# Hybrid decoder step on 8 cores: three small loads moved to ACT's queue, one tile load moved to GpSimd's queue, the second half of the down products placed after the last up product, and the last tile finished in halves

## The reference, cut to what matters

```python
def block(x, pool_ctx, pos, run_mlstm, norm1, w_in, b_gate, w_pool, pool_scale, head_gain, w_out, norm2, w_up, w_down):
    u, q, k, v, o, ig, lf = mixer_inputs(x, norm1, w_in, b_gate)      # rmsnorm(x) @ w_in, 1024 -> 2568
    u_ext = jnp.concatenate([pool_ctx.astype(u.dtype), u], axis=1)
    pool_out = pool_mix(u_ext, pos, w_pool, pool_scale)               # moving averages over 2, 4, 8, 16 rows
    h, mstate = run_mlstm(q, k, v, ig, lf)                            # matrix memory, chunk after chunk
    x = x + mixer_output(pool_out, h, o, head_gain, w_out, x.dtype)
    x = x + channel_mixer(x, norm2, w_up, w_down)                     # square(relu(rmsnorm(x) @ w_up)) @ w_down, 1024 -> 4096 -> 1024
    return x, u_ext[:, -POOL_CTX:], mstate
...
    y_prompt = rmsnorm(xp[:, N_META:], norm_f)
    y_sample = rmsnorm(xs, norm_f)
```

## Time and profile before

| | us |
|---|---|
| median of 3 runs (lowest to highest) | 813.78 (812.28 to 815.24) |
| the profiled execution, its own time | 813.62 |
| its span on the slowest core, core 5 | 812.6 |
| spans of the eight cores | 804.5 to 812.6 |
| PE busy on core 5 | 761.5 (94% of the span) |
| DVE, ACT, POOL busy | 425.9, 363.4, 156.9 |

### The profile page before, as it was taken

One profiled execution on the slowest core, in us unless ns is written; L12 is line 12 of the kernel. 1 busy time (PEld: TensorE's weight loads), 2 busy tenths in 40 slices (PEclk: granted clock), 3 DMA queues, 4 the chain that ended last, 5 costly groups with the idle time before them and its releaser, 6 DMA issues.

```text
span 812.6 us, 16660 instructions; the slowest of 8 cores (804.5 to 812.6 us)
## 1 busy us (share of the span) xinstructions
PE 761.5 (94%) x6707; PEld 529.1 (65%) x6707; DVE 425.9 (52%) x952; ACT 363.4 (45%) x867; POOL 156.9 (19%) x241
## 2 busy tenths in 40 slices
PE   0799899999999999999999799959999999999996
PEld 0477677878778788878798577628744444444442
DVE  0755886768768648768566665134323242421211
ACT  3455695776878536868637554103310010101011
POOL 6532430333312311202311301010000110000000
PEclk9999999999999999999999999979999999999999
DMA  8999994344344332332226799963355555553401
GB/s 165 175 199 178 184 189 94 92 85 92 91 112 99 62 103 58 87 117 79 66 78 92 159 187 280 224 138 105 99 214 186 202 200 202 164 187 118 186 34 53
DMA packets 35716, 110.43 MB, mean 136 GB/s; under 512 B 3415, under 2 KB 6855, under 8 KB 31654
## 3 DMA queue, kind: packets, MB, share of 16 engines
q1 hardware_dynamic: 21446, 63.64, 26.4%
q0 software_dynamic: 9504, 28.67, 22.1%
q10 hardware_dynamic: 4688, 17.04, 5.8%
HBM read 96.41 MB, written 39.64 MB: 167 GB/s over the span
## 4 chain that ended last, share of the span: by engine, by line
PE 81%; DMA 9%; DVE 5%; issue 2%; ACT 1%; POOL 1%; SPq 0%; POOLq 0%; DVEq 0%; ACTq 0%
PE B L428 79%; DMA wdn<-w_down 5%; PE B L431 2%; DMA xdn<-w_down 2%; DMA gvec<-gcols 2%; DMA C0b<-sC 1%; DVE zt L437 1%; DVE ast L434 0%; DVE xn2T L434 0%; DVE rows L441 0%; DVE wsm L441 0%; DVE xnT L434 0%; DVE Pt L434 0%; SPq L422 0%; POOL Wa L448 0%
## 5 line engine op out<-in xcount | busy, mean ns | idle before, releaser
L428 PE MATMUL B<-xn2T,wup 128*128 128x256 bf16 (+1 forms) x2304 | 247.3, 264 | 0.0
L428 PE MATMUL B<-wdn,aTl 128*128 128x512 bf16 (+1 forms) x952 | 213.8, 382 | 9.1 <-DMA xdn<-w_down 9.1
L428 PEld LDWEIGHTS B<-xn2T,wup 128*128 128x128 bf16 x2304 | 203.7, 98 | 23.4 <-issue 0.4
L428 PEld LDWEIGHTS B<-wdn,aTl 128*128 128x128 bf16 (+1 forms) x952 | 93.7, 99 | 120.9 <-DMA xdn<-w_down 9.2
L434 DVE TENSOR_TENSOR xt<-xt,B 128x512 f32<-128x512 f32 (+1 forms) x68 | 46.6, 685 | 183.7 <-PE B L428 183.4
L434 DVE TENSOR_TENSOR ast<-rr 128x512 bf16<-128x512 f32 x132 | 97.2, 736 | 74.6 <-ACT rr L425 58.4
L425 ACT ACTIVATE rr<-B 128x512 f32<-128x512 f32 x132 | 78.3, 593 | 112.5 <-PE B L428 66.9
L425 ACT ACTIVATE junk<-xt 128x1024 bf16<-128x1024 f32 (+1 forms) x17 | 18.0, 1057 | 196.3 <-DVE xt L434 196.3
L428 PE MATMUL B<-w_out_sb,mixT 128*128 128x512 bf16 (+1 forms) x272 | 64.2, 386 | 0.0
L448 POOL TENSOR_TENSOR kz<-ktm,wsm 64x512 bf16<-64x512 bf16 x16 | 16.7, 1059 | 167.2 <-PE B L428 155.5
L425 ACT ACTIVATE xn<-xt 128x1024 bf16<-128x1024 f32 (+2 forms) x34 | 35.8, 1052 | 22.7 <-DVE xt L434 20.2
(11 more groups left out here) (196 smaller groups left out, 932.3 us busy)
## 6 DMA issues: line engine op xcount, KB each, us to landing
aTd<-ast SPq DMA_DIRECT2D x32, 512.0 KB, 4.1
aTl<-aTd SPq DMA_DIRECT2D x16, 1024.0 KB, 4.9
wup<-w_up POOLq DMA_DIRECT2D x8, 1024.0 KB, 36.8
x2d<-xt SPq DMA_DIRECT2D x16, 512.0 KB, 3.8
xt<-x2d SPq DMA_DIRECT2D x16, 512.0 KB, 3.8
yp<-xt ACTq DMA_DIRECT2D x16, 512.0 KB, 2.6
wdn<-w_down POOLq DMA_DIRECT2D x7, 1024.0 KB, 14.0
xt<-xp SPq DMA_DIRECT2D x13, 512.0 KB, 4.8
```

The costliest lines, as they stand in the source:

```text
L428: return lambda: nc.tensor.matmul(out, lhsT=lhsT, rhs=rhs, start=start, stop=stop)
```

## The change

The loads of `gvec`, `earl` and `rowc` go from SP's queue to ACT's, ahead of everything else there, with a one-element exponential (`warm`) behind the first of them, which pulls the load of ACT's function table to the start. The load of prompt tile 1 goes from the head of SP's queue to GpSimd's (`XSW` 1). A key `upend` is written by the last up products and read by every PE operation on blocks 4 to 7, and by the load of the third `aTl`. The load of `gfB` (the last norm's gains) reads `wdn5`, and the loads of `C0f` for `csu(e)` read `dn{e}`, the end of down product e. The last tile's norm, scaling and store are split in two column halves, with a second store on SP. `POOLP` goes from 10 to 40 and `OGP` from 0 to 60.

```diff
@@ -19,7 +19,7 @@
 EPS = 1e-6
 WIN = (2, 4, 8, 16)
 UPV = 1800
-PRE, FRONT, MID, TAIL, POOLP, OGP = -50, -50, 30, -150, 10, 0
+PRE, FRONT, MID, TAIL, POOLP, OGP = -50, -50, 30, -150, 40, 60
 NBC = 5
 LOG = None
 
@@ -516,6 +516,7 @@
         colS = sb("colS", [80, 24])
         decr = sb("decr", [4, 16]); msr = sb("msr", [4, 16]); mpr = sb("mpr", [4, 1])
         mix_end = base[0]
+        warm = sb("warm", [1, 2])
 
         eo = [t_off["wup2"][0]]
 
@@ -554,6 +555,7 @@
 
 
         bank = pl.newbank
+        G(-5, lambda: nc.gpsimd.memset(warm[:, 0:1], 1.0), [], ['warm'], 0.1)
 
         def bk(b): return 'V%d' % b
 
@@ -561,9 +563,10 @@
         pl.place('xt0m', *pl.span['xt0'])
         pl.split('xt0', 'xt0m')
         DMA(0, 'sp', xt[0][64:80, :], meta[:, :], [], ['xt0m'], 'meta', 64e3)
-        DMA(0, 'sp', earl[:], early[:, :], [], ['earl'], 'earl', 64e3)
-        DMA(0, 'sp', gvec[:], gcols[:, :], [], ['gvec'], 'gvec', 10e3)
-        DMA(0, 'sp', rowc[:], rowin[:, :], [], ['rowc'], 'rowc', 1e3)
+        DMA(-3, 'act', gvec[:], gcols[:, :], [], ['gvec'], 'gvec', 10e3)
+        DMA(-2, 'act', earl[:], early[:, :], [], ['earl'], 'earl', 64e3)
+        DMA(-1, 'act', rowc[:], rowin[:, :], [], ['rowc'], 'rowc', 1e3)
+        A(-4, act(warm[:, 1:2], warm[:, 0:1], AF.Exp), ['warm'], ['warm2'], 1.5)
 
         def memset(prio, ap, v, key, cost, R=()):
             G(prio, lambda: nc.gpsimd.memset(ap, v), list(R), [key], cost)
@@ -680,7 +683,7 @@
         def scan(out, d, init, op0, op1):
             return lambda: nc.vector.tensor_tensor_scan(out=out, data0=d, data1=d, initial=init, op0=op0, op1=op1)
 
-        XSW = {2: 2.5, 3: 4.2, 4: 5.2}
+        XSW = {1: 1.5, 2: 2.5, 3: 4.2, 4: 5.2}
 
         def xload(pos):
             i = pos - 1
@@ -1036,7 +1039,7 @@
                         fns = []
                         for k in range(8):
                             fns.append(mm(B[b][:, hf * 256:(hf + 1) * 256], w_up_sb[fo][:, k, (f % 8) * 128:(f % 8 + 1) * 128], xn2T[gs][:, k, :], k == 0, k == 7))
-                        P(pr, fns, ['xn2T%d0' % gs, 'xn2T%d1' % gs, 'wup%d0' % fo, 'wup%d1' % fo], [bk(b)], 8 * mm_cost(256))
+                        P(pr, fns, ['xn2T%d0' % gs, 'xn2T%d1' % gs, 'wup%d0' % fo, 'wup%d1' % fo], [bk(b)] + (['upend'] if g == 7 and fo == 3 and fp == 3 else []), 8 * mm_cost(256))
                     av = a[:].rearrange("p t f c -> p f t c")[:, 2 * fp:2 * fp + 2, :, :]
                     r_ = rc[0] % 2; rc[0] += 1
                     A(pr - UPV, act(rr[r_][:], B[b][:], AF.Relu), [bk(b)], ['rr%d' % r_], cA(512))
@@ -1053,7 +1056,7 @@
                 for fi in range(8):
                     for k in range(8):
                         fns.append(mm(B[b][:, fi * 64:(fi + 1) * 64], w_up_sb[fo][:, k, fi * 128:(fi + 1) * 128], xn2T[0][:, k, 0:64], k == 0, k == 7))
-                P(pr, fns, ['xn2T00', 'wup%d0' % fo, 'wup%d1' % fo], [bk(b)], 64 * 0.034)
+                P(pr, fns, ['xn2T00', 'wup%d0' % fo, 'wup%d1' % fo], [bk(b)] + (['upend'] if fo == 3 else []), 64 * 0.034)
                 av = a[:, 0, 0:4, :].rearrange("p f c -> p (f c)")
                 r_ = rc[0] % 2; rc[0] += 1
                 A(pr - UPV, act(rr[r_][:], B[b][:], AF.Relu), [bk(b)], ['rr%d' % r_], cA(512))
@@ -1127,12 +1130,12 @@
         NC = 3
         C0f = [pbt("C0f%d" % i, [128, 8, 128]) for i in range(NC)]
         kz = [pbt("kz%d" % i, [64, 4, 128], BF16) for i in range(2)]
-        DMA(2400, 'sp', gfB[:], norm_f.partition_broadcast(128), [], ['gfB'], 'gfB', 512e3)
+        DMA(2400, 'sp', gfB[:], norm_f.partition_broadcast(128), ['wdn5'], ['gfB'], 'gfB', 512e3)
 
         def csu(e, pr):
             s = e % NC
             ck = 'C0f%d' % s
-            DMA(pr - 200, 'act', C0f[s][:], sCv[:, 8 * e:8 * e + 8, :], [], [ck], 'L' + ck, 512e3)
+            DMA(pr - 200, 'act', C0f[s][:], sCv[:, 8 * e:8 * e + 8, :], ['dn%d' % e], [ck], 'L' + ck, 512e3)
             for jj in range(2):
                 j = 2 * e + jj
                 z = kz[j % 2]; zk = 'kz%d' % (j % 2)
@@ -1144,6 +1147,8 @@
                       [ck, 'decS', bk(b)], [ck], 0.35)
             DMA(pr, 'act', Csv[:, 8 * e:8 * e + 8, :], C0f[s][:], [ck], ['o_C_s%d' % e], 'S' + ck, 512e3)
 
+        for half in range(2):
+            pl.place('xo%d' % half, t_off['xt3'][0] + 2048 * half, t_off['xt3'][0] + 2048 * half + 2048)
         order = list(range(8)) + [SP] + list(range(8, 16))
 
         def loads(n):
@@ -1154,7 +1159,7 @@
                 av = aTl[a][:].rearrange("p f c -> p (f c)")[:, 0:2048].rearrange("p (f c) -> p f c", c=64)
                 DMA(pr - 200, 'sp', av, aTs[:, :, :], ['aTs'], ['aTl%d' % a], 'LaTl%d' % a, 512e3)
             else:
-                DMA(pr - 200, 'sp', aTl[a][:], aTd[t], ['aTd%d' % (t // 2)], ['aTl%d' % a], 'LaTl%d' % a, 1024e3)
+                DMA(pr - 200, 'sp', aTl[a][:], aTd[t], ['aTd%d' % (t // 2)] + (['upend'] if n == 2 else []), ['aTl%d' % a], 'LaTl%d' % a, 1024e3)
             nr = 64 if t == SP else 128
             DMA(pr - 190, 'sp', xb[n % 3][0:nr, :], x2d[128 * t:128 * t + nr, :], ['x2d%d' % t], ['xt%d' % (n % 3)], 'x%d' % (n % 3), 512e3)
 
@@ -1169,13 +1174,29 @@
                 av = a[:].rearrange("p f c -> p (f c)")[:, 0:2048].rearrange("p (f c) -> p f c", c=64)
             else:
                 av = a[:]
+            last = n == 16
+            s_ = st[n % 2]; sk = 'st%d' % (n % 2)
             for half in range(2):
+                hc = slice(half * 512, (half + 1) * 512)
                 b = bank('D')
                 for q in range(2):
                     P(pr, [mm(B[b][r_, :], av[:, f, r_], wdn[f // 4][:, f % 4, half * 512:(half + 1) * 512], f == 0, f == 31) for f in range(16 * q, 16 * q + 16)],
-                      [ak] + ['wdn%d' % u for u in range(4 * q, 4 * q + 4)], [bk(b)], 16 * mm_cost(512))
+                      [ak] + (['upend'] if q else []) + ['wdn%d' % u for u in range(4 * q, 4 * q + 4)], [bk(b)] + (['dn%d' % n] if half and q else []), 16 * mm_cost(512))
                 V(pr - 1000, vtt(x_[r_, half * 512:(half + 1) * 512], x_[r_, half * 512:(half + 1) * 512], B[b][r_, :], ALU.add), [xk, bk(b)], [xk], cV(512))
-            s_ = st[n % 2]; sk = 'st%d' % (n % 2)
+                if last:
+                    A(pr - 1000, act(junk[:, hc], x_[:, hc], AF.Square, accum_out=s_[:, 2 + half:3 + half]), [xk], ['junk', sk], 0.8)
+                    V(pr - 1000, vtt(xt[3][:, hc], x_[:, hc], gfB[:, hc], ALU.mult), [xk, 'gfB'], ['xo%d' % half], 0.6)
+                    if half == 0:
+                        V(pr - 1000, vts(s_[:, 4:5], s_[:, 2:3], 1.0 / D, ALU.mult, EPS, ALU.add), [sk], [sk], 0.15)
+            if last:
+                A(pr - 1000, act(s_[:, 5:6], s_[:, 3:4], AF.Ln, scale=1.0 / D, bias=s_[:, 4:5]), [sk], [sk], 0.21)
+                A(pr - 1000, act(s_[:, 5:6], s_[:, 5:6], AF.Exp, scale=-0.5), [sk], [sk], 0.21)
+                V(pr - 1000, vts(xt[3][:, 0:512], xt[3][:, 0:512], s_[:, 5:6], ALU.mult), ['xo0', sk], ['xo0'], 0.4)
+                A(pr - 1000, act(xt[3][:, 512:1024], xt[3][:, 512:1024], AF.Copy, scale=s_[:, 5:6]), ['xo1', sk], ['xo1'], 0.6)
+                for half, q in ((0, 'sp'), (1, 'act')):
+                    DMA(pr, q, yp[128 * t:128 * t + 128, half * 512:(half + 1) * 512], xt[3][:, half * 512:(half + 1) * 512],
+                        ['xo%d' % half], ['o_yp%d%d' % (t, half)], 'xo%d' % half, 256e3)
+                return
             A(pr - 1000, act(junk[r_, :], x_[r_, :], AF.Square, accum_out=s_[r_, 2:3]), [xk], ['junk', sk], 1.25)
             rstd(pr - 1000, s_, sk, 2, nr)
             V(pr - 1000, vstt(x_[r_, :], x_[r_, :], s_[r_, 3:4], gfB[r_, :], ALU.mult, ALU.mult), [xk, sk, 'gfB'], [xk], 1.25)
```

## The result

The changed kernel takes 802.55 us (median of four runs, 802.31 to 802.81) against 814.51 us for the kernel before, run beside it. The ratio is 0.9858, with an interval from 0.9837 to 0.9878: 12.0 us faster. 797 us were forecast. So the sign and most of the amount came as said, and 5.5 us are missing.

The account below looks back on a forecast made before the run. PE's work bounds the kernel nearly everywhere. 812.6 - 2.0 - 2.7 - 11.6 + 0.5 - 1.1 + 0.5 = 796.2 us, plus 1.0 us for the execution's own time, gives 797 us; range 790 to 807 us.

Parts of the forecast that it names:

- the forecast's own case: Whole kernel: the forecast as it stands, 797 us, own range 791 to 802 us; chance 0.62.
- rival (a): At the start of the down products: the store of `ast` takes the place of `xdn`; 803 to 809 us; chance 0.20.
- The start: Start of the kernel: earlier small loads bring `xnT` and `tt` sooner; 2.0 us gained, between 0 and 3.6.
- Rival (c): At the kernel's start: the small loads stay as slow as they were; 800 us; chance 0.10.
- The wait for `Pt`: Near 467 us: more PE work ahead of the wait cuts it; 2.7 us gained, between 0 and 3.4.
- The start of the down products: Up matmuls now precede the wait for `xdn`: 9.1 us of wait and 2.5 us of low clock go, 11.6 us gained.
- The store of `ast`: Between the last up products and down products: a late store may stop PE; 0.5 us lost, between 0 and 12.
- The tail: Last add to last store: less square and scaling behind the last product; 1.1 us gained, between 0.7 and 1.6.
- The new order elsewhere: From 110 us on: `POOLP` and `OGP` shift the engines' order; 0.5 us lost, between 0 and 5.
- rival (d): In every prompt tile: the new order makes PE wait at `Pt` or `mixh`; over 814 us; chance 0.05.

Follow-up runs that it names:

- the priorities back: Changed kernel with `POOLP` and `OGP` put back to 10 and 0: 798.73 us, ratio 0.9832.
- The down part alone: Kernel before with only `upend` and the conditions on the third `aTl`, `gfB` and `C0f` loads: 7.7 us faster, 9.7 us in the mean of the cores.
- the one with only the `C0f` condition: Changed kernel with `POOLP` and `OGP` at 10 and 0 and, of the three conditions on loads, only that on `C0f`: ratio 0.9814.
- The mark alone: Kernel before with `upend` on the last up products and second-half down products, no conditions on the loads: 806.6 us, ratio 0.9926.
- priorities alone: Kernel before with only `POOLP` and `OGP` changed, to 40 and 60: ratio 0.9993.
- the changed kernel less its down part: Changed kernel without `upend` and without the conditions on the third `aTl`, `gfB` and `C0f` loads: ratio 0.9988.

## Why the prediction was right, and where it was off

The 802.5 us lie inside the stated range of 790 to 807 us, but half a microsecond above the 802 us to which the forecast's own case reached, and below the 803 us at which rival (a) began. The largest term of the sum, the down products, and that of the start came nearly as said; what kept the time from 797 us is mostly one small term, the last one below.

**The start**, 2.0 us forecast: 2.6 us by the time, 1.6 us in the mean of the cores. Each step came within 1 us: `xnT` done at 11.5 us, the `wo` product from 13.8 us (forecast 14.4), `tt` at 18.8 us (19.4). The 1.5 us by which `wo` was to land sooner did not follow from their own numbers (4.8 us less 2 or 3 is 1.8 to 2.8 us), and it was 2.2 us (11.2 us for 13.4 us). Rival (c) is refuted by the 2.1 us of `gvec`. What I had not seen is that the clock takes part of it back. PE, which began earlier and then waited for `wo` and `wk`, ran the next products at the lower of its two levels (1.2 GHz), as their durations show; from 20 to 45 us the granted clock is 0.80, for 0.93 before. After the change:

```profile
22.05 2.31 PE L428 MATMUL B<-xnT,wk 128*128 128x80 bf16 x32 [3.44 <-DMA wk<-w_in]
...
29.23 3.11 PE L428 MATMUL B<-xnT,wk 128*128 128x128 bf16 x32
...
36.69 1.90 PE L428 MATMUL B<-wv,xnT 128*128 128x512 bf16 x8 [2.63 <-DVE kT L445]
```

and before:

```profile
24.77 1.32 PE L428 MATMUL B<-xnT,wk 128*128 128x80 bf16 x32
...
29.62 1.95 PE L428 MATMUL B<-xnT,wk 128*128 128x128 bf16 x32
...
36.85 3.21 PE L428 MATMUL B<-wv,xnT 128*128 128x512 bf16 x8 [3.30 <-DVE kT L445]
```

The first product starts 2.7 us earlier and the second 0.4 us, and at `wv` the lead is 0.16 us. There the clock of before is low and that of after full, which gives back 1.3 us. The end is near the forecast; the way to it was not the one that I gave.

**The wait for `Pt`**, 2.7 us forecast: the 3.42 us wait is gone, but a wait of 1.77 us for `xt` at 458.61 us and the 1.50 us for `rr` came near it. By the busy time from 440 to 531.7 us the net is 1.3 us (87.53 less 86.24). Putting the priorities back brought the wait for `Pt` back and was faster all the same.

**The start of the down products**, 11.6 us forecast: the idle time and the low clock are both gone. The down part alone gives 9.7 us in the mean of the cores and 7.7 us in the time. The mechanism was right. That the slowest of eight cores gains less than the mean was not in the sum at all.

**The store of `ast`**, 0.5 us forecast, between 0 and 12: 1.50 us on PE in the changed kernel. The range was real and not caution: without the conditions, and with the new `OGP`, the profiled runs have waits of up to 11.4 and 4.2 us on it. The reason given, that the loads which leave this stretch make up for it, agrees with these two runs. With the old `OGP` the stores cost PE nothing even without the conditions.

**The tail**, 1.1 us forecast between 0.7 and 1.6: 0.8 us by the trace.

**The new order elsewhere** is the term that was off: "I read from the order no shorter distance between a product and its reader than before, and put the cost at 0.5 us, between 0 and 5". It measured 5.1 us of idle PE in the changed kernel (338.67 less 333.60 us), and 4.3 us between the two programs run side by side. That is at the upper bound given and ten times the size taken. It came by rival (d)'s mechanism, a wait at `mixh`, but once, near 164 us, with smaller ones behind it, and not in every tile. The order lists what comes after what; it does not show that the gate's result comes later on ScalarE, nor that a load with one buffer has only the time between two readers. With the measured sizes, and the forecast's own 11.6 us for the down products, the sum is 812.6 - 1.6 - 1.3 - 11.6 - 0.8 + 5.1 = 802.4 us of span, against 801.2 us in the trace. The 1.5 us of the store are within the 1.3 us; the 1.2 us left over I can't place. With the 9.7 us that the down part gave alone in the mean the sum would be 804.3 us, 3.1 us over the trace.

The kernel with the priorities back, 798.7 us, is by its median the fastest here (the one with only the `C0f` condition, at 0.9814, can't be told from it), and near what was forecast for the whole change.

## What to carry to other kernels

Moving ready work in front of a late load took away the whole wait and the low clock after it. The mark alone gave 6.1 us in the mean of the cores, and with conditions on the loads behind it 9.7 us: look for what stands next on the engines and the queues. An early load does not only take bandwidth. It also lets its reader into the order, and here that reader, DVE's update of `C0f`, stopped PE for 2.1 us on every core. In the order with the new `OGP`, where a late store could reach PE, leaving the conditions out cost 8 to 11 us. A stretch in which the bounding engine has 1.3 us of idle time in 340 can only lose, so a priority that reorders it needs a run of its own and not a term of half a microsecond. On eight cores the time is the slowest core's: look at the mean span over the cores beside it, since a loss on a few cores of each run can cost nearly all of the gain (0.9988) while the mean still shows it (7.1 us).

## What the runs showed of the hardware that was not expected

A load of 10 KB took 16.1 us from issue to landing behind other loads on SyncE's queue, and 2.1 us as the first DMA on ScalarE's. The same kind of store of `a` lands after 3.0 us at best and 27.2 us at worst on one core between 440 and 560 us (priorities alone), where the DMA engines are busy for 0.9 to 1.0 of the time up to 545 us. Holding back 0.5 MB loads on ScalarE's queue brought the longest of these stores, on SyncE's, from 16.6 to 22.8 us down to 11.4 to 14.4 us over the eight cores. Over the eight cores of one run the spans have a standard deviation of 2.6 us before, and of 5.9 us in the changed kernel less its down part (the mean of that deviation over the runs that count).
